# Final states of two retention heads moved from the mixer into the fifth expert pair, a tail in quarters, and smaller transfers for the fifteenth pair

## The reference, cut to what matters

```python
# mixer of one layer, for 256 prompt rows and 8 decode rows (heads H=4, RET_DK=256, RET_DV=512, D=1024)
proj = x_normed @ w_in                       # cb, cc, ch, q, k, v, g, ga, gb
scores = (q @ k.T) * decay_mask              # per head, prompt rows
out    = scores @ v
S_new  = (k * k_decay).T @ v                 # final state of a prompt head -> ret_prompt[h]
S_dec  = gamma_h * S + k_row.T @ v_row       # 4 heads x 8 decode rows -> ret_sample
merged = sigmoid(ga) * (conv @ w_a) + sigmoid(gb) * (retention @ w_b)
h = x + merged @ w_o
# mixture of experts: 32 experts, top 4 of each row
hid = xb @ w1[e] + b1[e]
act = (clip(up) + 1) * gate * sigmoid(1.702 * gate)
y   = act @ w2[e] + b2[e]
h = h + sum over the row's experts of gate_weight * y
y_prompt, y_sample = rmsnorm(h, norm_f)
```

## Time and profile before

| | us |
|---|---|
| three runs | 1416.67 median (1416.41 to 1417.35) |
| the profiled execution | 1416.43 |
| its span (first to last instruction) | 1414.6 |
| mixer, to the last wb projection | 7 to 452.6 |
| out projection, routing, first gather | 452.6 to 499.0 |
| 16 expert pairs | 499.0 to 1400.95 |
| tail | 1400.95 to 1414.6 |

### The profile page before, as it was taken

One profiled execution on the slowest core, in us unless ns is written; L12 is line 12 of the kernel. 1 busy time (PEld: TensorE's weight loads), 2 busy tenths in 40 slices (PEclk: granted clock), 3 DMA queues, 4 the chain that ended last, 5 costly groups with the idle time before them and its releaser, 6 DMA issues.

```text
span 1414.6 us, 17229 instructions
## 1 busy us (share of the span) xinstructions
PE 1348.2 (95%) x7181; PEld 701.9 (50%) x7181; DVE 387.4 (27%) x712; ACT 252.1 (18%) x375; POOL 95.8 (7%) x166
## 2 busy tenths in 40 slices
PE   8999999999999999999988989989999898998997
PEld 6667678888887443443333433323333342332332
DVE  4235443642501422222211211113211132121223
ACT  1233343320000421111111111011110111101112
POOL 1122212210000210000000000000000000000000
PEclk9999999999999999999999999999999999999999
DMA  9888879874524699999999999999999999999996
GB/s 351 345 302 306 300 263 343 309 280 145 188 94 185 254 415 429 430 431 431 430 431 430 433 431 432 435 433 432 430 430 433 431 432 434 433 433 429 425 428 278
DMA packets 44467, 519.95 MB, mean 368 GB/s; under 512 B 5338, under 2 KB 5898, under 8 KB 22884
## 3 DMA queue, kind: packets, MB, share of 16 engines
q1 hardware_dynamic: 29984, 470.59, 79.2%
q0 software_dynamic: 12896, 45.70, 9.4%
q10 hardware_dynamic: 1540, 2.99, 0.6%
HBM read 497.63 MB, written 21.67 MB: 367 GB/s over the span
## 4 chain that ended last, share of the span: by engine, by line
PE 68%; DMA 27%; DVE 3%; issue 1%; SPq 1%; ACT 1%; POOL 0%; DVEq 0%; POOLq 0%; ACTq 0%
PE bank L1941 25%; DMA ring<-in_w_pairs 25%; PE bank L1602 19%; PE bank L1901 4%; PE bank L1650 4%; PE bank L1993 3%; PE bank L1887 3%; PE bank L1747 2%; DMA arena<-in_state_ret 2%; PE bank L1619 1%; PE bank L1939 1%; SPq L678 1%; PE bank L1897 1%; PE bank L1970 1%; PE bank L1653 1%
## 5 line engine op out<-in xcount | busy, mean ns | idle before, releaser
L1941 PE MATMUL bank<-ring,arena 128*64 128x512 f32 x1536 | 351.9, 609 | 29.4 <-DMA ring<-in_w_pairs 29.4
L1602 PE MATMUL bank<-arena,ring 128*128 128x264 f32 x1472 | 331.5, 387 | 0.4 <-DVE arena L1193 0.4
L1602 PEld LDWEIGHTS bank<-arena,ring 128*128 128x128 f32 x1472 | 278.7, 190 | 51.0 <-issue 3.1
L1941 PEld LDWEIGHTS bank<-ring,arena 128*64 128x64 f32 x1536 | 111.2, 140 | 248.4 <-issue 230.4
L1993 PE MATMUL bank<-ring,arena 128*64 128x512 f32 x768 | 171.8, 594 | 6.2 <-DMA ring<-in_w_pairs 6.1
L1941 PE MATMUL bank<-arena 128*64 128x512 f32 x512 | 118.2, 616 | 12.2 <-DMA arena<-in_w_pairs 12.2
L1993 PEld LDWEIGHTS bank<-ring,arena 128*64 128x64 f32 x768 | 55.1, 137 | 109.0 <-issue 99.4
L1528 DVE TENSOR_SCALAR arena<-bank 128x512 f32<-128x512 f32 x32 | 22.1, 691 | 272.5 <-PE bank L1941 272.5
L1941 PEld LDWEIGHTS bank<-arena 128*64 128x64 f32 x512 | 36.9, 141 | 85.3 <-issue 68.5
L1551 DVE COPY arena<-bank 64x512 f32<-64x512 f32 x32 | 21.9, 683 | 181.3 <-PE bank L1993 181.3
L1518 DVE TENSOR_TENSOR hs<-hs,bank 128x256 f32<-128x256 f32 x16 | 6.7, 421 | 222.1 <-PE bank L1897 222.1
(11 more groups left out here) (253 smaller groups left out, 993.1 us busy)
## 6 DMA issues: line engine op xcount, KB each, us to landing
ring<-in_w_pairs SPq DMA_DIRECT2D x58, 4096.0 KB, 27.9
arena<-in_w_pairs SPq DMA_DIRECT2D x20, 4096.0 KB, 29.3
ring<-in_w_mixer SPq DMA_DIRECT2D x58, 1024.0 KB, 9.0
ring<-in_w_pairs SPq DMA_DIRECT2D x26, 2048.0 KB, 13.2
arena<-in_state_ret POOLq DMA_DIRECT2D x32, 512.0 KB, 8.1
out_ret_sample<-arena POOLq DMA_DIRECT2D x32, 512.0 KB, 6.0
arena<-in_w_pairs SPq DMA_DIRECT2D x6, 2048.0 KB, 14.5
arena<-v_decode POOLq DMA_DIRECT2D x32, 256.0 KB, 6.8
```

The lines of the kernel that those rows point to most:

```text
L1602: ins = pe.matmul(bank[:, 0:T], weight(n + k // 4, k % 4)[:, 128 * j:128 * (j + 1)], rhs[:, k, :], start=k == 0, stop=k == KD * groups - 1)
L1941: ins = pe.matmul(out, xgT[:, k, 64 * e:64 * (e + 1)], held(n, 2 * D * (k % W1_KS) + c), start=False, stop=k == KD - 1)
```

## The change

1. The final states of heads 0 and 1 (`LATE`) leave the mixer: no `kt` and no `st` for them, but `save`, which writes their values and their keys (still in rows of dk, `kT`) to device memory. SP reads them back (`load_end`), with the `tail` rows and `norm_f`, in front of pair 4's weights. In pair 4 (`LATE_PAIR`) TensorE transposes the keys (`turn_late`), ScalarE scales them, and TensorE makes the states (`late_states`); SP stores them after the last weights.
2. `STEP_EVERY` goes from 6.2 to 5.0 and `VALUES_TO_STEP` from 18 to 14; after the last `prep` two of the closing events of a head may follow one piece of work.
3. The last expert's second layer is made in four quarters of columns, from a new layout of its weights: a quarter is columns 128q to 128q+127 of both halves, and two pieces of 512 KB hold it. Each quarter is copied, combined, added and squared by itself (two products of 256 columns).
4. Pair 14 (the fifteenth) is loaded in 2 MB transfers, and the second layer of pair 15's first expert in pieces of 512 KB too.

The diff, cut:

```diff
 def is_wide(pair):
-    return SPARE_PAIRS <= pair < PAIRS - 1
+    return SPARE_PAIRS <= pair < PAIRS - 2
@@
+    by_columns = w2[-1, -1].reshape(128, KD, 2, QUARTERS, 128).transpose(0, 3, 1, 2, 4)
+    out[-1, -1].reshape(by_columns.shape)[...] = by_columns
@@
+LATE = (0, 1)
+LATE_PAIR = 4
-STEP_EVERY = 6.2
+STEP_EVERY = 5.0
-VALUES_TO_STEP = 18.0
+VALUES_TO_STEP = 14.0
@@ def mixer_order
-        main.extend([... (("qs", h), 0.0), (("kt", h), 0.5), (("sc", h), 1.4), (("v", h, 1), 7.0)])
+        main.extend([... (("qs", h), 0.0)])
+        if h in DEFERRED:
+            main.append((("kt", h), 0.5))
+        main.extend([(("sc", h), 1.4), (("v", h, 1), 7.0)])
-        main.append((("save", h), 0.0) if h in DEFERRED else (("st", h), 3.6))
+        main.append((("save", h), 0.0))
...
-        if ends:
-            order.append(ends.pop(0))
+        for _ in range(2 if n == H * NS else 1):
+            if ends:
+                order.append(ends.pop(0))
@@ block.sync
-                    if number == PAIRS - 1 and n >= PAIR_CHUNKS - W2_CHUNKS:
+                    if number == PAIRS - 1 and n >= PAIR_CHUNKS - 2 * W2_CHUNKS:
...
+            def load_end(it):
+                used(it, PAIR_CHUNKS - 1)
+                sp.dma_start(same_row, a["tail"][:, 0:128]).then_inc(end_in, 16)
+                sp.dma_start(nfs, a["tail"][:, 128:384]).then_inc(end_in, 16)
+                sp.dma_start(nfb, a["norm_f"]....to_broadcast([128, D])).then_inc(end_in, 16)
+                sp.wait_ge(saved, SAVED)
+                for i in range(len(LATE)):
+                    sp.dma_start(k_late[i], k_late_dram[:, 2 * i:2 * i + 2, :]).then_inc(end_in, 16)
+                    sp.dma_start(v_late[i], v_late_dram[i]).then_inc(end_in, 16)
             def load_rest(r):
-                for pair in range(1, 4):
+                for pair in range(1, LATE_PAIR):
                     load_pair(r * PAIRS + pair, pair, pair)
+                load_end(r * PAIRS + SPARE_PAIRS - 1)
...
-            sp.wait_ge(up_done, 2 * PAIRS * rounds)
-            sp.dma_start(slots[0][:, 0:384], a["tail"]).then_inc(tail_in, 16)
-            sp.dma_start(nfb, a["norm_f"]....to_broadcast([128, D])).then_inc(tail_in, 16)
...
+            sp.wait_ge(kept_read, 2 * len(DEFERRED) + LATE_READS * rounds)
+            for i, h in enumerate(LATE):
+                sp.dma_start(o["ret_prompt"][0, 0, h]..., v_late[i]).then_inc(kept_out, 16)
@@ block.scalar
-                        if t == 0 and h >= 1:
-                            if h == H - 1: ac.wait_ge(st_out, ...)
-                            else: was_filled(ac, ("st", h - 1, 1))
+                        if t == 0 and h >= 2:
+                            ac.wait_ge(saved, SAVED_LATE)
...
+                    if h in LATE:
+                        ac.dma_start(v_late_dram[LATE.index(h)], values[h]).then_inc(saved, 16)
+                        if h == LATE[0]:
+                            ac.wait_ge(qk_ready, 4 * len(LATE))
+                            ac.dma_start(k_late_dram, kT[:, :, 0:LP]).then_inc(saved, 16)
+                        continue
...
+                def turn_late():
+                    for i in range(len(LATE)):
+                        ac.wait_ge(late_done, LATE_READS * r + i + 1)
+                        for t in range(2):
+                            at = C_KDEC + 2 * LATE[i] + t
+                            ins = ac.activation(k_late[i][:, t, :], psum[i][:, DK * t:DK * (t + 1)], ACT.Copy, scale=cst[:, at:at + 1])
+                        ins.then_inc(kept_read, 1)
+                def late_states(i):
+                    ac.wait_ge(late_done, LATE_READS * r + len(LATE) + 2 * i + 2)
+                    for g in range(2):
+                        ac.activation(v_late[i][:, g, :], psum[g][:, :], ACT.Copy).then_inc(kept_read, 1)
...
+            for t in range(2):
+                ac.wait_ge(added, ADDS * PAIRS * rounds + t + 4)
+                square(t, QUARTERS - 1)
+                ac.wait_ge(mean3, rounds)
+                ac.activation(stat[:, 8 + t:9 + t], sums3[:, t, LAST_SUM:LAST_SUM + 1], ACT.Sqrt,
+                              bias=sums3[:, t, REST_SUM:REST_SUM + 1]).then_inc(root3, 1)
@@ block.vector
+                        if (name, g, j) == ("k", 1, 1):
+                            v.wait_ge(saved, SAVED_LATE)
...
+            def last_columns(r, it):
+                for q in range(QUARTERS):
+                    quarter_is_done(v, r, it, q)
+                    v.tensor_copy(ysb[64:128, 128 * q:128 * (q + 1)], psum[QUARTER_BANKS[q]][0:64, 128 * q:128 * (q + 1)])...
+                    if q >= 1:
+                        add_quarter(r, it, q - 1)
+                v.wait_ge(combined, ADDS * it + 3)
+                v.tensor_tensor(hs[:, :], hs[:, :], psum[ADD_BANKS[0]][:, 0:256], ALU.add).then_inc(added, 1)
+                v.wait_ge(quarter_squared, SQUARES * r + 2 * SQUARES)
+                v.reduce_sum(sums3[:, :, REST_SUM:REST_SUM + 1], sums3[:, :, 0:EPS_SUM + 1], AX.X).then_inc(mean3, 1)
+                add_quarter(r, it, QUARTERS - 1)
@@ block.tensor
+                def last_columns():
+                    for q in range(QUARTERS):
...
+                        for f in range(KD):
+                            if f % 4 == 0: ... wait for the piece
+                            for side in range(2):
+                                ins = pe.matmul(psum[QUARTER_BANKS[q]][64 * side:64 * (side + 1), 128 * q:128 * (q + 1)], lhs,
+                                                slots[slot_of(number, n)][:, at:at + 128], start=False, stop=f == KD - 1)
+                        if q in (1, 2):
+                            combine_quarter(q - 1)
+                    combine_quarter(2)
+                    ... hs product, 4 x 256 columns
+                    combine_quarter(3)
+                def turn_late():
+                    pe.wait_ge(end_in, END_LOADS + END_LOADS * r)
+                    for i in range(len(LATE)): ... 4 transposes of k_late[i] into psum[i]
+                def late_states(i):
+                    pe.wait_ge(kept_read, 2 * len(DEFERRED) + len(LATE) + 2 * i + LATE_READS * r)
+                    for g in range(2):
+                        for t in range(2):
+                            ins = pe.matmul(psum[g][:, :], k_late[i][:, t, 128 * g:128 * (g + 1)], v_late[i][:, t, :], ...)
+                        ins.then_inc(late_done, 1)
                 first_layer(1, range(4, KD))
+                if late:
+                    turn_late()
                 second_layer(0, range(0, 4))
+                if late:
+                    late_states(0)
                 turn_acts(1)
                 second_layer(0, range(4, KD))
-                second_layer(1, range(0, KD))
+                if late:
+                    late_states(1)
+                if last:
+                    last_columns()
+                else:
+                    second_layer(1, range(0, KD))
```

More of the change, by code:

```diff
@@ new lines, in expert_pair @@
+                    for t in range(2):
+                        ac.wait_ge(added, ADDS * it + ADDS + t + 1)
+                        square(t, 2)
+                with ac.Fori(0, LATE_PAIR) as pair:
+                    expert_pair(pair)
+                expert_pair(LATE_PAIR, late=True)
+                with ac.Fori(LATE_PAIR + 1, PAIRS - 1) as pair:
+                    expert_pair(pair)
+                expert_pair(PAIRS - 1, last=True)
+            ac.wait_ge(added, ADDS * PAIRS * rounds + 3)
@@ L1537, in activate, with expert_pair @@
                 v.tensor_tensor(acts, ucl, sig, ALU.mult).then_inc(act_ready, 1)
-            def expert_pair(r, pair, first=False):
+            def expert_pair(r, pair, first=False, last=False):
                 it = r * PAIRS + pair
```

277 lines of the change are left out of this document (181 added, 96 removed).

## The result

The changed kernel took 1420.16 us (median of 20 runs, 1416.63 to 1422.57), the kernel before beside it 1416.91 (20 runs, 1416.26 to 1418.95): ratio 1.0018, 95% interval 1.001 to 1.0026. The forecast was 1412.0 with 1408.3 to 1417.0: a gain was predicted, and there is a small loss. The profiled execution took 1419.33 us, its span is 1417.5 (1414.6 before).

What follows compares the result with a forecast made beforehand. The prediction took TensorE to bound the mixer and the DMA byte stream the experts, with a tail behind. Terms -7.4 + 5.3 + 0.7 - 0.5 + 0.2 - 3.0 = -4.7 us gave 1412.0 us, range 1408.3 to 1417.0.

Steps and rivals of the forecast that it cites:

- Mixer, -7.4: Mixer: two heads' states leave TensorE, 7.9 us less work, with 0.5 us more idle time; -7.4 us.
- I take +0.5: Mixer: TensorE's added idle time under the denser work list, +0.5 us between bounds of -1.4 and +11.
- Rival S: Mixer: the state chain becomes the bound, TensorE waits 11 us, the sum is +5.8, 1422.5 us; chance 0.12.
- Bytes in the stream, +5.3: Ahead of pair 4's weights: 2.29 MB of added loads at 431 GB/s delay every later weight; +5.3 us.
- TensorE in pair 4, 0: Pair 4: the 7.9 us of state work returning to TensorE is covered by queued transfers; cost 0.
- Pair 14, +0.7: Pair 14: 2 MB transfers run at 427 GB/s instead of 432 for 4 MB ones; +0.7 us.
- End of the stream, -0.5: Last weights: `tail` and `norm_f` no longer follow the last pieces, 1 MB more of stores do; -0.5 us.
- the pieces of pair 15's first expert: 0: Pair 15: loading the first expert's second layer in 512 KB pieces costs nothing; 0.
- Lateness at the last piece, +0.2: Last expert's second layer: two early combines fit between arriving quarters, making TensorE only 0.2 us late.
- Rival Q: End: 128-column products cost 0.110 us each, the layer 14 us, TensorE 6 us late; +1.3, 1418.0 us; chance 0.10.
- Tail, -3.0: After the last piece lands: quarter-wise combining and scaling shorten the tail from 14.75 to 11.7 us; -3.0 us.

Runs made afterwards that it cites:

- four_bufs: The changed kernel with a fourth state buffer and each decode state loaded one step earlier; 1414.61 us.
- after_again: The changed kernel, unaltered, timed and profiled a second time; 1419.43 us.
- no_work: four_tail_wide without the transposes, scalings and products of the states of heads 0 and 1 in pair 4, their loads kept; 1412.81 us.
- first_2mb: four_tail_wide with the second layer of pair 15's first expert loaded in two 2 MB transfers again; 1413.04 us.
- tail_loads_last: The changed kernel with `tail` and `norm_f` loaded behind the last weights again; 1417.12 us.
- no_gather: The changed kernel without the gather of a next pair's rows in the last pair; 1418.36 us.
- pieces_1mb: first_2mb with each quarter of the last expert in one 1 MB transfer instead of two of 512 KB; 1412.64 us.
- four_tail_wide: The changed kernel with a fourth state buffer, `tail` and `norm_f` behind the last weights, and pair 14 in 4 MB transfers again; 1412.62 us.

## Why the prediction was wrong, step by step

**Mixer, -7.4: the step that failed most.** The work that leaves TensorE was priced right: with four buffers the mixer ends 7.7 us earlier. What failed is "I take +0.5" for the idle time, between bounds of -1.4 and +11; it was 4.06 us in one profile and 5.2 in the other, where before had 1.4. Its argument was "a load of 8.1 plus a store of 6.0 over three buffers is 4.7 us a step". That sum takes medians, while the kernel before had loads of 17.3 us too. It also gives the load three steps: by the order in which GpSimd issues, a load and the work on it have two, and the load of 12.18 us made them 16.3 us long, 8.2 a step, where the new list wants 7.24. In the changed kernel the loads' median rose to 9.7 and the stores' to 8.2; why is open. Against four_bufs, whose gaps are 0.89 us, the mixer ends 4.7 us later: 3.2 are the gaps, 0.75 the start, and 0.8 no row accounts for. In after_again the lower clock behind the longest gap adds some 1.5 us, a term that the forecast did not have. Rival S, "the state chain becomes the bound of the mixer", is what happened, though the idle time came to less than half of its 11 us, so the mechanism was named and given 0.12. Its test row (TensorE waiting for VectorE between 140 and 300 us) is half there: the largest gap stands at 122.07.

**Bytes in the stream, +5.3: the mechanism right, the size low by 0.8.** 4.3 for keys and values, 1.8 for `tail` and `norm_f`, 6.1 against bounds of 5.3 to 5.8, with 0.5 of scatter. By the packets' own time in the changed kernel's trace it is 4.0 and 1.9: the forecast took the rate of 32 KB rows for rows of 0.5 to 4 KB. Of the 2.29 MB, 0.72 need not have been there.

**TensorE in pair 4, 0: right** (no_work). **Pair 14, +0.7:** 0.3.

**End of the stream, -0.5: failed,** with "the pieces of pair 15's first expert: 0". From TensorE's start on pair 15's third chunk to L both kernels take 44.5 us, so the two terms together are 0. Pieces of 512 KB run at 406 to 411 GB/s, and the change doubles their number, which first_2mb puts at 0.3 us and the rates at 0.5. The 395 GB/s of the last 15 us before was put down to `tail` and `norm_f`; tail_loads_last shows no delay from them in the changed kernel.

Of the 7.1 us between S and L, 6.1 + 0.3 leave 0.7 that no term and no run accounts for. They lie ahead of that third chunk, where the small pieces play no part; two profiles of one kernel differ by up to 0.5.

**Lateness at the last piece, +0.2: failed, 1.8 measured.** The premise was that "the two early combines, 0.9 us each, fall between quarters that arrive 2.4 us apart". It ignores that TensorE had next to no idle time in which to fit them. The windows from TensorE's start on the third chunk of pair 15 to the end of its products, before and after:

```profile
1355.20:1400.95 45.75, 45.41 (x251) 17.33 (x251) 10.83 (x17) 5.32 (x8) 0.61 (x2) 1.00 0.99 412
```

```profile
1359.40:1406.87 47.47, 47.47 (x362) 23.65 (x362) 13.37 (x24) 8.11 (x20) 0.87 (x3) 1.00 0.96 393
```

Two combines of 1.06 us less 0.34 of idle time are 1.8. Nor would idle time ahead of them have been enough: a quarter with its combine takes 3.0 us and arrives in 2.6, and no_gather, with 3.2 us less to do, is still 2.2 us behind L. Rival Q named the place, TensorE late at the end, but not the cause: a quarter's 32 instructions took 1.75 us, as the forecast assumed. That the forecast's 0.054 us for each, half way between two other shapes, came out at 0.055 is luck; no row fixed it.

**Tail, -3.0: right**, 10.63 us from the end of the products instead of 13.65. Of this 1.8 went back as lateness, so 1.2 reached the end.

Together: 4.4 + 1.6 + 1.6 = 7.6 us between the -4.7 predicted and the +2.9 found. The range reached to 1417.0 because it held the failure of one term; three stretches failed with one sign.

## What to carry to other kernels

When a producer of work leaves the critical engine, ask what the next chain does in its worst case, not its median: take the longest load of the trace and see whether a list that is denser by the planned amount has a buffer for it. Count the steps that the program's order of issue leaves to a load, not the buffers. A buffer more was worth 5.0 us here and the planned gain of the mixer came out in full. Work that is put "between arrivals" is free only if the engine has idle time there in the row and keeps up with the arrivals afterwards; and an engine that is 99% busy ahead of the end turns both a shorter tail and an earlier landing into nothing.

## What the runs showed of the hardware

**Size of a transfer in a full queue.** The stream ran at 432 GB/s in transfers of 4 MB, 424 to 429 in 2 MB, 415 to 419 in 1 MB (pieces_1mb, 1380 to 1390 us) and 406 to 411 in 512 KB, at a DMA share of 0.99 to 1.03. In these traces the transfers of the weights consist of packets of 32, 16, 8 and 4 KB, one row each, with mean times of 1216, 617, 313 and 164 ns on one engine; over 16 engines that makes 431, 425, 418 and 400 GB/s. So the row length alone could account for the rates; no run changed it without the size of the transfer. By the Trainium skill, "DMA: Bandwidth & Descriptors", Bandwidth, a transfer of 1 MB, measured with issues from GpSimd, reaches 341 GB/s, 78% of the peak, and the advice is to batch to 1 MiB or more. The direction agrees; the size does not carry over, since transfers of 1 MB and of 512 KB that are queued behind each other lose 3 to 6% against those of 4 MB here, not a fifth. These were issued from SP.

**Products of 128 columns with 64-wide weights.** 32 instructions in 1.75 us are 55 ns each. By the Trainium skill, "TensorE: Matmul & The Clock Gate", Back-to-back issue gap, a stream of weight loads and matmuls at 128 columns is paced at about 81 ns; by the same section's formula for the isolated gap of a single matmul it would be about 56. The rows agree with the second, for pairs of instructions that write the two halves of a bank.

**One idle time and the clock.** TensorE idled 5.9 to 7.8 us at pair 4 in each kernel that reads the keys and values back there. Its next 32 instructions, 7.03 to 7.09 us elsewhere, took longer; four_tail_wide, and then the window around the idle time in it:

```profile
706.08 9.54 PE L2056 MATMUL bank<-arena 128*64 128x512 f32 x32 [5.92 <-DMA arena<-in_w_pairs]
```

```profile
690.00:715.00 25.00, 18.59 (x78) 6.23 (x76) 1.37 (x2) 1.19 (x2) 0.49 (x2) 0.86 1.03 438
```

The granted clock was 0.86 over 25 us, so for a part of them TensorE had 1.2 GHz instead of 2.4. It cost 2.5 us of TensorE, and the stream ran on at a DMA share of 1.03, so none of the time that the trace shows. The length of the idle time alone does not give the price: the same 32 instructions took 8.47 us behind 7.64 us in the changed kernel, 8.78 behind 2.78 in the kernel before (at 1291.92), and 7.09 behind 1.66 (at 708.41). Where TensorE sets the pace, as in the mixer of after_again, such a fall adds to the time.
